# Weights, states and tables stored in device memory in the order in which the partitions read them

## Chip, cores and metric

One core of one Trainium2 chip. The metric is device time in microseconds (us) of one execution, lower is better. It covers the program on the device; what `kernel()` does with arrays on the host before and after is no part of it.

## The reference, cut to what matters

One step of a one-layer hybrid decoder for a prompt of 512 tokens and 8 sample sequences of 8 tokens each, all in fp32, width 1024:

```python
h = RMSNorm(x)
z, xbc, dt, q, kv_c, kv_s, kv_w, nsa_g, br_g = split(h @ w_in)       # 1024 x 9040
y_ssm, conv_new, ssm_new = mamba(z, causal_conv(xbc, state_conv), dt, state_ssm)   # 32 heads, state 128
o_attn, win_new = nsa(q, kv_c, kv_s, kv_w, caches, page_table)       # 16 heads, 2 KV groups
merged = sigmoid(g_ssm) * (y_ssm @ w_ssm_branch) + sigmoid(g_attn) * (o_attn @ w_attn_branch)
x = x + merged @ w_out
x = x + PEER(RMSNorm(x))     # q = h @ peer_wq, scores against peer_sub_keys, 128 experts per token:
                             # out = sum_k gelu(h . peer_u[e_k]) g_k peer_v[e_k],  e_k among 16384
y = RMSNorm(x)
```

Outputs are y, the new key and value rows, the new convolution tails (3 rows of 3072 columns for the prompt and for each sequence) and the new recurrent states (32 heads x 64 x 128 for the prompt and for each sequence).

## The kernel before, in words

Tokens stand in 5 tiles: 0 to 3 hold the prompt, 128 tokens each, and tile 4 the 64 sample tokens. `build` (L3647) runs the chain of stages norm, conv, ssd, zgate, branch, kv, qk, cmp, attn, branch, out, query twice: for group "a" (tiles 0 and 1) and for group "b" (tiles 2, 3 and, for the projections, 4). In names of tiles and tensors the last letter is the group. Then come stages for the sample alone (state, mix, branch, pages, cmp, attn, branch, out, query), and at the end `rest`. Each stage is a Block: all engines meet at its end.

**Weights.** `Weights` cuts the matrices into pieces of [128 partitions x 2048 floats], 1 MB each, and SP loads them in the order of use (`feed`, L3623) into slots: 16 for group a (2 of `wb`, 14 in the ring of the experts, which is idle then), the 2 of `wb` for group b. A slot's next load is issued when the PE has used the piece in it. In DRAM the matrices lie row after row, so that one partition's part of a piece is made of short runs: 1 KB for 256 columns of `w_in`, `w_attn_branch` and `peer_wq`, 512 B for the 128 columns of `w_ssm_branch` (L3588), 256 B for the 64 columns of a query head, where a piece takes 4 DMAs (L3600), 4 KB for `w_out`. The sample's own stages load 2 MB at a time into `wb` and `room` (L2208, L2904, L3007), in runs of 4 or 2 KB.

**Experts.** `Experts` (L3112) interleaves, from group b on, the expert rows of earlier tiles with the stages: 576 gathers of `peer_u` and 576 of `peer_v`, an indirect DMA from GpSimd each (L3314), 128 rows of 4 KB = 0.5 MB, into a ring of 14 slots `e_ring`. The VectorE takes a `u` slot with one dot product (L3463), the PE four `v` slots with 16 matmuls (L3381). How many of them each stage carries is fixed by `k.share`; the stages' hooks (`ex.pe(i)`, `ex.dve(i)`, ...) place them between the stage's own instructions. A gather is issued when the slot 14 places before it has been read. Weights go through DMA queue 1 (issued by SP), gathers through queue 0 (issued by GpSimd).

**Norm** (a): norm weights and convolution weights are loaded as rows, `vec_a` and `vec_b`, and turned by the PE into the columns `vcol` (L277, L255).

**Conv** (b): for each of 24 channel tiles f, the PE projects (L379, 8 matmuls of 320 columns) and turns the old tail from `zs`/`sigs` rows into PSUM (L384); ACT copies to SBUF (L503 to L508); the VectorE convolves and copies the new tail (L561, L562); ACT applies Silu; the PE turns the output (L400) and the new tail (L403); ACT copies both out (L454 to L458). The tails leave as rows from SBUF (L359).

**Ssd** (b): 8 units; the VectorE adds each unit's state into `h` (L824). At the end the PE turns all of `h` in 16 transposes (L750), ACT copies them (L790), and SP stores them in one DMA and waits for it (L844).

**Query** (a): sub keys are loaded as rows (L1719), turned by 16 transposes (L1750) between the second and third projection, copied by ACT (L1808), and stored as `keys_scratch`, from which group b and the sample load them. Scores (L1769) feed the ranking on the VectorE.

**State** (sample): 16 head pairs, in each 0.5 MB of `state_ssm` in and 0.5 MB out, both in runs of 512 B (L1895, L1901), through 8 slots.

Of the kernel before, what the change touches and what calls it, by code (L numbers as in the profile page):

```python
# [116 lines left out]
def stage_norm(nc, k, g):  # L117

    with ExitStack() as ctx:
# [9 lines left out]
        if g.first:  # L129
            vec_a, vec_b = sb("vec_a", [32, P]), sb("vec_b", [120, P])  # L130
            table, part = sb("table", [P, NB], I32), sb("part", [P, 1], I32)
            tablef, partf = sb("tablef", [P, NB]), sb("partf", [P, 1])
            vec_in, table_in, const_set, consts_done, vec_turned, a_done = (
                sem(n) for n in ("vec_in", "table_in", "const_set", "consts_done", "vec_turned", "a_done"))
# [6 lines left out]
        def _(sp):  # L141
# [5 lines left out]
            for dst, src in (  # L147
                (vec_a[0:8, :], k.norm_mix_w[0].rearrange("(a p) -> a p", p=P)),
                (vec_a[8:16, :], k.norm_ffn_w[0].rearrange("(a p) -> a p", p=P)),
                (vec_a[16:32, :], k.ssm_norm_w[0].rearrange("(a p) -> a p", p=P)),  # L150
                (vec_b[0:24, :], k.conv_b[0].rearrange("(a p) -> a p", p=P)),
                (vec_b[24:120, :], k.conv_w[0].rearrange("w (a p) -> (w a) p", p=P)),
# [59 lines left out]
        def _(act):  # L212
# [10 lines left out]
            if g.first:  # L223
                act.wait_ge(vec_in, 16 * 8)
# [3 lines left out]
        def _(dve):  # L228
# [64 lines left out]
def stage_conv(nc, k, g):  # L293


    with ExitStack() as ctx:  # L296
# [13 lines left out]
        TURNS = F if g.sample else B_TILES  # L310
        per = WB // P
        NTP = len(g.prompt)
        if g.sample:
            cin_s = sb("in_s", [P, 2, NB, CONV_W - 1 + DS])
            tail = sb("tail", [P, 2, 27])
            ends_bc = k.sigs[:].rearrange("p a f n -> p (a f n)")[0:27]
            state_in, written = sem("state_in"), sem("written")

        def ends(f, r):

            if f < X_TILES:
                return k.zs[0:r, f * P:f * P + P]
            return ends_bc[0:r, (f - X_TILES) * P:(f - X_TILES) * P + P]
# [25 lines left out]
        def _(sp):  # L349
            if g.sample:  # L350
                state = k.state_conv[0].rearrange("b w c -> (b w) c")
                sp.dma_start(k.zs[0:24, :], state[:, 0:D_INNER]).then_inc(state_in, 16)
                sp.dma_start(ends_bc[0:24, :], state[:, D_INNER:]).then_inc(state_in, 16)
            k.w.feed(sp)
            if g.sample:
                sp.wait_ge(gathered, F)
                after = k.new_conv_sample[0].rearrange("b w c -> (b w) c")
                for src, cols in ((k.zs, slice(0, D_INNER)), (ends_bc, slice(D_INNER, CONV_DIM))):
                    sp.dma_start(k.new_conv_prompt[0, 0][:, cols], src[0:3, :]).then_inc(written, 16)  # L359
                    sp.dma_start(after[:, cols], src[3:27, :]).then_inc(written, 16)  # L360
                sp.wait_ge(written, 64)
# [9 lines left out]
        def _(pe):  # L371
            def project(f):
# [8 lines left out]
                if g.sample:  # L381
                    if f == 0:
                        pe.wait_ge(state_in, 32)
                    last = nc.tensor.transpose(k.ps[:, f % 2, N:N + 24], ends(f, 24), k.ident[0:24, 0:24])  # L384
                last.then_inc(projected, 1)

            def turn(f):
# [3 lines left out]
                if f < B_TILES:  # L391
                    pe.wait_ge(activated, f + 1)
                    for i, t in enumerate(g.tiles):
# [3463 lines left out]
```

## Time and profile before

| what | value |
|---|---|
| median of 3 runs | 3231.45 us (3214.28 to 3235.7) |
| profiled execution, own time | 3234.93 us |
| its span in the trace | 3233.2 us |
| PE busy / VectorE / ScalarE / GpSimd | 2217.7 / 1543.3 / 616.9 / 1492.6 us |
| DMA packets, bytes | 401016, 843.89 MB, mean 261 GB/s |
| queue 0 (gathers), share of 16 DMA engines | 644.95 MB, 54.6% |
| queue 1 (SP), share of 16 DMA engines | 229944 packets, 196.89 MB, 20.4% |

By the first matmul of each stage, group a ends at 708.4 us, group b at 1960.8 us, and the sample's stages and `rest` take what is left. A packet in the profile is one contiguous piece of a DMA. "Share" is the mean busy share of the core's 16 DMA engines, so 0.91 of a stage of 143.8 us is 130.9 us of work for all 16. A row "A <- B: t, n, m" of the waits says that A sat idle t us in n times, the longest m, until B was done.

### The profile page before, as it was taken

Reading aid. Unit: us, or ns where it says so; the run is one execution under the profiler, and the core shown is the slowest. Engines: PE = TensorE matmul, PEld = TensorE weight load, DVE = VectorE, ACT = ScalarE, POOL = GpSimd, SP = SyncE. Lnnn points to the kernel's source line nnn. Section 1 sums busy time; section 2 is a strip of 40 time slices with the busy share of each in tenths; the row PEclk is TensorE's granted clock in tenths of the full one; section 3 lists DMA queues with packets and bytes.
Section 4 is the critical chain, followed back from the end, with each engine's and each line's share of the span. In section 5 each row is a group of like instructions: output and inputs, shape, how many; then the busy total and the mean of one; then the engine's idle time right before and its main releaser. Section 6 shows DMA issues by size and latency. Waiting matters only on the chain. (4 is left out here: it accounts for less than half of the span.)

```text
span 3233.2 us, 32111 instructions
## 1 busy us (share of the span) xinstructions
PE 2217.7 (69%) x11116; PEld 1403.4 (43%) x11116; DVE 1543.3 (48%) x3888; ACT 616.9 (19%) x1746; POOL 1492.6 (46%) x1509
## 2 busy tenths in 40 slices
PE   8999979869777678756688894653446777564044
PEld 7788846556555466422235362332114443111000
DVE  4410042276888751256520065998535665108720
ACT  3330053113331100013340012321001111000000
POOL 0200000053254664457754357657555665443775
PEclk9999969879978888877899996655668898777567
DMA  6234602437637997889989978968988998997998
GB/s 218 79 92 121 140 26 78 130 111 236 204 102 257 332 325 263 266 325 350 350 308 290 349 250 287 352 221 284 412 344 325 352 389 304 314 340 288 339 370 316
DMA packets 401016, 843.89 MB, mean 261 GB/s; under 512 B 71194, under 2 KB 236914, under 8 KB 398181
## 3 DMA queue, kind: packets, MB, share of 16 engines
q0 software_dynamic: 170912, 644.95, 54.6%
q1 hardware_dynamic: 229944, 196.89, 20.4%
q8 instruction: 90, 1.47, 0.2%
q14 instruction: 70, 0.57, 0.1%
HBM read 821.54 MB, written 24.33 MB: 262 GB/s over the span
## 5 line engine op out<-in xcount | busy, mean ns | idle before, releaser
L3314 POOL DMA_INDIRECT e_ring<-in_peer_u,e_idx x576 | 692.2, 1202 | 542.9 <-DVE e_dot L3463 267.4
L3463 DVE CUSTOM_DVE_ANT_0 e_ring<-e_ring,e_h 128x1024 f32<-128x1024 f32 x576 | 703.0, 1254 | 175.4 <-DMA e_ring<-in_peer_u,e_idx 82.4
L3314 POOL DMA_INDIRECT e_ring<-in_peer_v,e_idxT x576 | 583.4, 1013 | 440.3 <-PE ps L3381 178.1
L3381 PE MATMUL ps<-e_ring,e_wz 128*32 128x512 f32 x2304 | 361.5, 742 | 297.1 <-DMA e_ring<-in_peer_v,e_idxT 261.3
L3381 PEld LDWEIGHTS ps<-e_ring,e_wz 128*32 128x32 f32 x2304 | 76.8, 125 | 507.2 <-issue 502.4
L1672 POOL CAST ra_atf<-ra_at 128x32 f32<-128x32 uint32 x8 | 1.7, 211 | 259.7 <-DVE ra_hit L1665 259.7
L379 PE MATMUL ps<-hTb,wb 128*128 128x320 f32 x384 | 112.1, 447 | 1.9 <-DMA wb<-in_w_in 1.9
L1957 PE MATMUL ps<-ss_bsel,ss_xde 64*128 64x512 f32 x64 | 54.6, 947 | 63.1 <-DVE room L2007 27.5
L1004 PE MATMUL ps<-hTb,wb 128*128 128x320 f32 x256 | 77.3, 462 | 16.9 <-DMA wb<-in_w_in 9.6
L379 PEld LDWEIGHTS ps<-hTb,wb 128*128 128x128 f32 x384 | 73.7, 197 | 30.8 <-issue 2.9
L1507 DVE TENSOR_REDUCE apb_nmax<-ps 128x2 f32<-128x768 f32 (+1 forms) x32 | 34.9, 1089 | 105.9 <-PE ps L1431 55.3
L1012 PE MATMUL ps<-xnatb,wb 128*128 128x256 f32 x256 | 66.9, 427 | 24.2 <-DMA wb<-in_w_ssm_branch 24.2
L3506 DVE TENSOR_TENSOR e_x<-e_x,ps 128x512 f32<-128x512 f32 x10 | 6.4, 683 | 155.9 <-PE ps L3381 113.4
L888 PE MATMUL ps<-hTb,wb 128*128 128x320 f32 x256 | 76.8, 456 | 0.0
L1092 POOL MEMSET inda<- 128x256 f32 x1 | 0.3, 312 | 163.6 <-POOLq L3707 163.6
L1012 PEld LDWEIGHTS ps<-xnatb,wb 128*128 128x128 f32 x256 | 55.1, 218 | 36.0 <-DMA wb<-in_w_ssm_branch 25.8
L1004 PEld LDWEIGHTS ps<-hTb,wb 128*128 128x128 f32 x256 | 51.5, 204 | 43.5 <-issue 14.9
L1760 PE MATMUL ps<-hTb,wb 128*128 128x256 f32 x256 | 61.1, 393 | 7.5 <-DMA wb<-in_peer_wq 4.7
L1189 PE MATMUL ps<-hTb,wb 128*128 128x320 f32 x160 | 48.3, 464 | 24.2 <-DMA wb<-in_w_in 17.6
L379 PE MATMUL ps<-hTa,e_ring 128*128 128x256 f32 x288 | 64.9, 379 | 0.0
L656 POOL TENSOR_TENSOR sa_xdt<-xnata,dt 128x512 f32<-128x512 f32 x8 | 8.4, 1044 | 121.3 <-POOLq L296 104.0
L888 PEld LDWEIGHTS ps<-hTb,wb 128*128 128x128 f32 x256 | 50.5, 203 | 20.0 <-issue 3.7
(720 smaller groups left out, 4329.9 us busy)
## 6 DMA issues: line engine op xcount, KB each, us to landing
wb<-in_w_in SPq DMA_DIRECT2D x38, 1024.0 KB, 5.3
e_ring<-in_w_in SPq DMA_DIRECT2D x24, 1024.0 KB, 5.3
wb<-in_peer_wq SPq DMA_DIRECT2D x10, 1024.0 KB, 5.4
wb<-in_w_ssm_branch SPq DMA_DIRECT2D x9, 1024.0 KB, 6.1
e_ring<-in_peer_u,e_idx POOLq DMA_INDIRECT x576
e_ring<-in_peer_v,e_idxT POOLq DMA_INDIRECT x576
e_ring<-in_w_ssm_branch SPq DMA_DIRECT2D x7, 1024.0 KB, 5.8
wb<-in_w_in SPq DMA_DIRECT2D x24, 256.0 KB, 4.3
```

Of the source, the lines that this page charges most:

```text
L379: last = nc.tensor.matmul(k.ps[:, f % 2, 0:N], w[:, kk, c:c + P], k.hT[:, kk, 0:N], start=(kk == 0), stop=(kk == KD - 1))
L656: gp.tensor_tensor(v3(xdt), x3, by_head(k.dt[:, t0 + c, hs], P), ALU.mult).then_inc(xdt_done, 1)
L888: last = mm(k.ps[:, f % 2, 0:N], w[:, kk, :], k.hT[:, kk, 0:N], start=(kk == 0), stop=(kk == KD - 1))
L1004: last = mm(k.ps[:, b, 0:N], w[:, f, :], k.hT[:, f, 0:N], start=(f == 0), stop=(f == KD - 1))
L1012: last = mm(k.ps[:, b + 1, 0:NP], w[:, f, :], src_p(f), start=(f == 0), stop=(f == depth - 1))
L1189: last = nc.tensor.matmul(k.ps[:, i % 4, 0:N], w[:, f, :], k.hT[:, f, 0:N], start=(f == 0), stop=(f == KD - 1))
L1507: v.tensor_reduce(nmax[:, 2 * d:2 * d + 2], k.ps[:, 0:2, 0:width(d)], AX.X, ALU.max, negate=True).then_inc(maxed, 1)
L1760: last = mm(k.ps[:, i % 2, 0:NP], w[:, f, :], k.hT[:, f, 0:NP], start=(f == 0), stop=(f == KD - 1))
L1957: mm(k.ps[:, 2 + q % 2, :], xde[:, f * P:f * P + P], bsel[:, j % 2, seqs(i), :].rearrange("p b n -> p (b n)"), start=True, stop=True).then ...
L3314: nc.gpsimd.indirect_dma_start(out=self.ring[:, place % self.NR, :], out_offset=None, in_=k.peer_u if kind == "u" else k.peer_v, in_offset ...
L3381: last = nc.tensor.matmul(k.ps[32 * b:32 * b + 32, self.SUMS + i, :], self.wz[:, at:at + 32], self.ring[:, self.v_at[n] % self.NR, 512 * i ...
L3463: v.tensor_tensor_reduce(uu, uu, self.h[:, tile % 2, :], 1.0, 0.0, ALU.mult, ALU.add, self.dot[:, tile % 2, t:t + 1]).then_inc(self.dotted, 1)
```

## The change

`kernel()` now hands over, beside the other inputs, arrays in the order in which the program reads them: all pieces of the weights as `weights[n]`, [128, 2048], so that a partition's part of a piece is one run of 8 KB; the sample's copies as `late_weights[n]`, [128, 4096], runs of 16 KB; the five vectors as `columns` [128, 152]; the sub keys turned; `state_ssm` as [16, 128, 1024] with runs of 4 KB, and the same for the new states; the window cache with runs of 4 KB; the convolution states by channel. New states and tails of prompt and sample are stored as they lie in SBUF and put into the reference's order on the host. The on-chip turns of vectors, sub keys, tails and prompt state go.

```diff
@@ Weights
-        for n, loads in enumerate(self.pieces):
-            self.total[n % self.slots] += 16 * len(loads)
+        for n in range(len(self.pieces)):
+            self.total[n % self.slots] += 16
...
-        for i in range(HPK // 2):
-            add([(lambda t, side=side, j=j: pair(t, side, j),
-                  w_view(k.w_in, COL_Q + (side * HPK + 2 * i + j) * HD, HD)) for j in range(2) for side in range(KVH)])
...
-            for part, src in self.pieces[n]:
-                sp.dma_start(part(self.places[n % self.slots]), src).then_inc(self.sem[n % self.slots], 16)
+            width = self.pieces[n]
+            sp.dma_start(self.places[n % self.slots][:, 0:width],
+                         self.k.weights[n][:, 0:width]).then_inc(self.sem[n % self.slots], 16)
@@ stage_norm
-                (vec_a[0:8, :], k.norm_mix_w[0].rearrange("(a p) -> a p", p=P)),
...
+                (k.vcol[:], k.columns),
...
-                    dve.wait_ge(vec_turned, 1)
-                    own(v.tensor_copy(k.vcol[:, 0:32], k.ps[:, 6, 0:32]))
-                    own(v.tensor_copy(k.vcol[:, 32:152], k.ps[:, 7, 0:120]))
+                    dve.wait_ge(vec_in, 16 * 4)
@@ stage_conv
-                sp.wait_ge(gathered, F)
...
+                sp.wait_ge(tailed, F)
+                sp.dma_start(k.new_conv_prompt, k.ctail[:].rearrange("p f t -> p (f t)")).then_inc(written, 16)
+                sp.dma_start(k.new_conv_sample, after.rearrange("p f b t -> p (f b t)")).then_inc(written, 16)
...
-                if g.sample:
-                    if f == 0:
-                        pe.wait_ge(state_in, 32)
-                    last = nc.tensor.transpose(k.ps[:, f % 2, N:N + 24], ends(f, 24), k.ident[0:24, 0:24])
...
-                if g.sample:
-                    pe.wait_ge(tailed, f + 1)
-                    last = nc.tensor.transpose(k.ps[0:27, b, 3 * P:4 * P], tail[:, f % 2, :], k.ident[:])
...
-                    last = a.copy(ends(f, 27), k.ps[0:27, b, 3 * P:4 * P])
...
-                    last = a.copy(cin_s[:, f % 2, :, 0:3], src[:, N:N + 24].rearrange("p (b t) -> p b t", b=NB))
+                    if f == 0:
+                        act.wait_ge(state_in, 16)
+                    last = a.copy(cin_s[:, f % 2, :, 0:3], before[:, f])
@@ stage_ssd
-                        last = nc.tensor.transpose(k.ps[:, q, i * P:i * P + P], h[:, f * P:f * P + P], k.ident[:])
...
-                sp.wait_ge(h_copied, 4)
-                sp.dma_start(k.new_ssm_prompt[0, 0].rearrange("h p n -> (h p) n").rearrange("(f q) n -> q f n", q=P),
-                             hout).then_inc(h_stored, 16)
-                sp.wait_ge(h_stored, 16)
+                for gr in range(GROUPS):
+                    sp.wait_ge(updated, U - GROUPS + gr + 1)
+                    sp.dma_start(k.new_ssm_prompt[:, channels(gr)], h[:, channels(gr)]).then_inc(h_stored, 16)
+                sp.wait_ge(h_stored, 16 * GROUPS)
@@ stage_sample_state
-                sp.dma_start(h0[f % NH0], view(k.state_ssm, f)).then_inc(h0_in[f % NH0], 16)
+                sp.dma_start(h0[f % NH0], k.state_before[f].rearrange("p (b n) -> p b n", b=NB)).then_inc(h0_in[f % NH0], 16)
@@ stage_sample_branch
-                for dst, part in load_w(wp[i % 2], w, i):
-                    sp.dma_start(dst, part).then_inc(wp_in[i % 2], 16)
+                sp.dma_start(k.room[i % 2], k.late_weights[first + i]).then_inc(wp_in[i % 2], 16)
```

The PE's instructions in conv of group b, before (L379 projects, L384 turns the old tail, L400 the output, L403 the new tail):

```order
L379 MATMUL ps<-hTb,wb 128x320 x8
L384 MATMUL ps<-ident,zs 128x24
L379 MATMUL ps<-hTb,wb 128x320 x8
L384 MATMUL ps<-ident,zs 128x24
L400 MATMUL ps<-ident,cb_out 128x128 x2
L400 MATMUL ps<-ident,cb_out 64x128
L403 MATMUL ps<-ident,cb_tail 27x128
L379 MATMUL ps<-hTb,wb 128x320 x8
```

and the same place of the changed kernel:

```order
L383 MATMUL ps<-wb,hTb 64x32 x8
L358 MATMUL ps<-hTb,wb 128x320 x16
L374 MATMUL ps<-ident,cb_out 128x128 x2
L374 MATMUL ps<-ident,cb_out 64x128
L358 MATMUL ps<-hTb,wb 128x320 x8
```

The two small turns of each channel tile are gone; the order of the rest is the same.

The PE's instructions at the end of ssd in group b, before (L720 and L727 belong to the last units, L895 and L888 to zgate):

```order
L708 MATMUL ps<-sb_xdt,zs 128x64 x8
L720 MATMUL ps<-h,mTb 128x512
L727 MATMUL ps<-sigs,Bnatb 128x512
L750 MATMUL ps<-ident,h 128x128 x16
L615 UNCONDITIONAL_BRANCH
L878 UNCONDITIONAL_BRANCH
L895 MATMUL ps<-ident,xnatb 128x128 x2
```

In the changed kernel the row L750 is missing, and nothing else moves there. SP's loads in kv and qk of group b, before (64 columns: one of the 4 DMAs of a query piece):

```order
L3634 DMA wb<-in_w_in 128x8x256
L3634 DMA wb<-in_w_in 128x8x48
L3634 DMA wb<-in_w_in 128x8x64 x8
L1068 UNCONDITIONAL_BRANCH
L1166 UNCONDITIONAL_BRANCH
L3634 DMA wb<-in_w_in 128x8x64 x12
```

and of the changed kernel:

```order
L3558 DMA wb<-in_weights 128x2048
L3558 DMA wb<-in_weights 128x384
L3558 DMA wb<-in_weights 128x2048 x2
L1017 UNCONDITIONAL_BRANCH
L1115 UNCONDITIONAL_BRANCH
L3558 DMA wb<-in_weights 128x2048 x5
```

The loads stand in the same order, one DMA to a piece. GpSimd's instructions are the same in both kernels.

## Rows read from the trace of the kernel before

**Rows 1.** Windows view by stage: length, busy time of each engine, granted clock, DMA share, GB/s.
```profile
0.00:708.40 708.40, 609.54 (x2905) 488.89 (x2905) 216.13 (x683) 196.03 (x566) 71.06 (x143) 0.90 0.37 104
723.80:883.00 159.20, 138.12 (x616) 97.08 (x617) 121.09 (x385) 51.91 (x210) 45.47 (x44) 0.92 0.70 226
1099.60:1243.40 143.80, 109.83 (x404) 83.63 (x405) 68.40 (x125) 8.56 (x23) 79.66 (x60) 0.84 0.91 312
1243.40:1376.90 133.50, 103.34 (x464) 67.03 (x464) 31.02 (x52) 9.16 (x35) 61.00 (x61) 0.87 0.84 265
1691.10:1801.40 110.30, 92.01 (x437) 57.05 (x433) 6.77 (x16) 4.53 (x20) 43.65 (x49) 0.92 0.91 288
1960.80:2164.50 203.70, 133.24 (x448) 75.59 (x449) 174.13 (x429) 58.20 (x165) 135.24 (x121) 0.64 0.96 324
2250.40:2304.30 53.90, 23.72 (x75) 7.02 (x77) 32.85 (x60) 1.45 (x5) 35.33 (x31) 0.69 1.03 410
2778.20:3233.20 455.00, 186.50 (x968) 48.05 (x968) 162.53 (x442) 22.01 (x54) 258.28 (x268) 0.70 0.90 335
```

**Rows 2.** DMA view of 1126 to 1130 us: packets, MB, share of the 16 engines.
```profile
q0 software_dynamic: 341, 1.23, 78.9%
q1 hardware_dynamic: 341, 0.35, 24.9%
```

**Rows 3.** DMA view of 1102 to 1104 us, where queue 1 stores an 8 KB row per partition.
```profile
q1 hardware_dynamic: 92, 0.49, 62.3%
```

**Rows 4.** DMA view of 17 to 120 us: loads with 1 KB runs, no gathers.
```profile
q1 hardware_dynamic: 19007, 19.17, 59.5%
```

**Rows 5.** DMA view of 335 to 345 us: loads with 256 B runs, no gathers.
```profile
q1 hardware_dynamic: 4160, 1.05, 59.3%
```

**Rows 6.** DMA views of 1100 to 1243, 1243 to 1376 and 1692 to 1801 us, queue 1.
```profile
q1 hardware_dynamic: 18847, 12.16, 28.6%
q1 hardware_dynamic: 24916, 8.54, 27.8%
q1 hardware_dynamic: 6712, 7.96, 26.9%
```

**Rows 7.** Waits of the engines from 1100 to 1243 us: total, times, longest.
```profile
PE ps L1012 <- DMA wb<-in_w_ssm_branch: 24.2, 4, 8.8
PE ps L1004 <- DMA wb<-in_w_in: 7.9, 2, 5.4
```

**Rows 8.** Waits from 1244 to 1376 us.
```profile
PE ps L1189 <- DMA wb<-in_w_in: 17.6, 1, 17.6
```

**Rows 9.** Waits from 1692 to 1801 us.
```profile
PE ps L1012 <- DMA wb<-in_w_attn_branch: 14.8, 3, 5.2
```

**Rows 10.** Waits from 2251 to 2304 us and from 2779 to 3010 us.
```profile
PE ps L2223 <- DMA wb<-in_w_ssm_branch: 24.8, 2, 20.0
PE ps L2223 <- DMA wb<-in_w_attn_branch: 13.9, 1, 13.9
```

**Rows 11.** Windows view of 1126.5 to 1131.5 us, just behind a wait for weights.
```profile
1126.50:1131.50 5.00, 5.00 (x12) 4.01 (x13) 0.00 (x0) 0.00 (x0) 1.88 (x2) 0.50 1.04 394
```

**Rows 12.** Groups of instructions from 723.8 to 883 us, shapes apart.
```profile
L384 PE MATMUL ps<-ident,zs 24*128 24x24 f32 x16 | 3.8, 239 | 0.0
L403 PE MATMUL ps<-ident,cb_tail 128*27 128x128 f32 x24 | 6.8, 283 | 8.2 <-DVE cb_tail L562 8.2
```

**Rows 13.** Timeline of TensorE around 628 us: start, length, instruction.
```profile
628.28 1.04 PE L1750 MATMUL ps<-ident,ra_sk 128*128 128x128 f32 x8
631.37 0.71 PE L1769 MATMUL ps<-ra_skT,ra_qT 128*128 128x128 f32 x4 [0.68 <-ACT ra_skT L1808]
```

**Rows 14.** Timeline of VectorE around 973 us.
```profile
972.89 0.68 DVE L824 TENSOR_TENSOR h<-h,ps 128x512 f32<-128x512 f32 x1
983.57 1.23 DVE L3463 CUSTOM_DVE_ANT_0 e_ring<-e_ring,e_h 128x1024 f32<-128x1024 f32 x1 [10.00 <-PEq L615]
```

**Rows 15.** Waits of GpSimd in the whole span.
```profile
POOL e_ring L3314 <- DVE e_dot L3463: 312.7, 112, 11.5
```

More of the change, by code:

```diff
@@ L314, in stage_conv @@
             cin_s = sb("in_s", [P, 2, NB, CONV_W - 1 + DS])
-            tail = sb("tail", [P, 2, 27])
-            ends_bc = k.sigs[:].rearrange("p a f n -> p (a f n)")[0:27]
             state_in, written = sem("state_in"), sem("written")
[L319 to L323, printed above, removed]
+            before, after = (k.zs[:, D * i:D * i + F * NB * (CONV_W - 1)].rearrange("p (f b t) -> p f b t", f=F, b=NB)
+                             for i in range(2))
         NT, t0 = len(g.tiles), g.tiles[0]
@@ L537, in convolve @@
                     dve.wait_ge(activated, f - 1)
-                    if g.sample:
-                        dve.wait_ge(turned, f - 1)
                 ap = acc[:, f % 2, 0:NP]
@@ L743, in _ @@
                     ex.pe(2 * u + 1)
-            if g.sample:
-                pe.wait_ge(updated, U)
-                pe.wait_ge(y_half, U)
-                for q in range(4):
-                    for i in range(4):
-                        f = 4 * q + i
-                        last = nc.tensor.transpose(k.ps[:, q, i * P:i * P + P], h[:, f * P:f * P + P], k.ident[:])
-                    last.then_inc(h_turned, 1)
         @block.scalar
@@ L785, in _ @@
                     ex.act(2 * u + 1)
-            if g.sample:
-                act.wait_ge(diag, U)
-                for q in range(4):
-                    act.wait_ge(h_turned, q + 1)
-                    a.copy(hout[:, 4 * q:4 * q + 4, :],
-                           k.ps[:, q, :].rearrange("p (i n) -> p i n", i=4)).then_inc(h_copied, 1)
         @block.vector
@@ L1717, in store @@
                 sp.dma_start(k.scores_dram[t0][:, i, :], s[:, i % NS_BUF, 1, :]).then_inc(s_out[i % NS_BUF], 16)
-            sp.dma_start(*((sk[:], keys) if g.first else (skT[:], k.skT_dram))).then_inc(sk_in, 16)
+            sp.dma_start(skT[:], k.keys_turned).then_inc(sk_in, 16)
             for i in range(HC):
@@ L1804, in _ @@
                     a.copy(qT[:, i % 2, :], k.ps[:, i % 2, 0:NP]).then_inc(q_copied, 1)
-                if i == 1 and g.first:
-                    for q in range(HC // 4):
-                        act.wait_ge(sk_turned, q + 1)
-                        a.copy(skT[:, 4 * q:4 * q + 4, :],
-                               k.ps[:, 2 + q % 2, :].rearrange("p (i n) -> p i n", i=4)).then_inc(sk_copied, 1)
                 if i:
@@ L2167, in stage_sample_mix, with stage_sample_branch @@
         ex.close()
-def row_chunk(dst, w, i):
-    return [(dst, w[512 * i:512 * i + 512, :].rearrange("(f p) n -> p f n", p=P))]
-def head_chunk(dst, w, i):
-    return [(dst[HD * g:HD * g + HD], w.rearrange("(g j d) n -> g d j n", g=KVH, d=HD)[g][:, 4 * i:4 * i + 4])
-            for g in range(KVH)]
-def stage_sample_branch(nc, k, name, w, depth, load_w, src, which):
+def stage_sample_branch(nc, k, name, first, depth, src, which):
     with ExitStack() as ctx:
```

245 lines of the change are left out of this document (119 added, 126 removed).

## The prediction

> **What bounds the kernel now.** I read the windows view stage by stage first. In group a, the first 708.4 us, TensorE works 609.5 us, the DMA share is 0.37 and no gathers run [rows 1]: here the PE sets the time, and faster loads buy nothing. From group b on the gathers run, and most stages show a DMA share of 0.84 to 1.03 [rows 1]. In the branch stage, 143.8 us, the PE works 109.8 and the DMA engines 0.91 x 143.8 = 130.9 us; both attention projections and the late stages look alike. State is different: VectorE works 174.1 of 203.7 us.
>
> The waits come second. In branch the PE waits 24.2 + 7.9 = 32.1 us for pieces of weights [rows 7], in kv and qk once for 17.6 us, for a query piece [rows 8], in the attention's branch 14.8 us [rows 9], in the sample's branch stages 24.8 and 13.9 us [rows 10].
>
> The DMA view tells why. At 1126 to 1130 us both queues moved 341 packets: they take turns, one packet for one packet, whatever a packet holds [rows 2]. So gathers with 4 KB packets got 1.23 MB through and weights, in runs of 1 KB, 0.35 MB: 88 GB/s, which makes a piece of 1 MB last 12 us, and one in runs of 512 B twice that, while the PE needs about 7 us for 16 matmuls of 427 ns. Where nothing contends, runs of 1 KB move 19.17 MB in 0.595 x 103 us of all engines, 19.5 GB/s an engine [rows 4]; runs of 256 B move 1.05 MB in 5.9 us, 11 GB/s an engine [rows 5]; the one place with 8 KB rows, a store beside gathers, shows 62.3% of the engines for queue 1 and 0.49 / (0.623 x 2 x 16) = 24.6 GB/s an engine [rows 3], 394 GB/s for 16. That is the nearest row for the new layout.
>
> So long runs do two things: a piece costs the engines less (1 MB: 2.7 us of all 16 instead of 3.4 with 1 KB and 5.9 with 256 B), and, which matters more, it arrives sooner beside gathers (1 MB at 0.49 MB in 2 us: 4.3 us, instead of 12 or more). With 8 KB packets a piece is never late for a PE that needs 7 us for one, unless its slot comes free late: each slot waits for the PE's use of the piece before, and two slots are enough for 4.3 us.
>
> A rule speaks against half of this. The Trainium skill, "DMA: Bandwidth & Descriptors", section Specifications, gives 512 B as the smallest transfer for full rate; by it only the 256 B pieces and the states' smallest rows would gain throughput. Rows 4 disagree, 19.5 against 24.6 GB/s at 1 KB, though not by much. What it would make of the time is rival 3.
>
> **The change part by part.** The sum is made against the profiled execution's own time, 3234.93 us (span 3233.2), which is 3.5 us over the median of the runs shown.
>
> Start-up (vectors as one load, no turns): two turns of the nearest row's size, 0.28 us each [rows 12], and two copies go, and the one load in place of several must still land first. 0 taken; -2 to +2.
>
> Key turns in group a's query: the PE goes from L1750 at 628.28 to the first scores at 631.37 us [rows 13]: the two quarters of turns seen there and the copy behind them go, and 631.37 - 628.28 = 3.1 us with them. **3**; 2 to 4. The keys of group b already come turned; their runs change little, 0.
>
> Conv of group b: out go 24 turns of the old tail at 239 ns and 24 of the new at 283 ns, 5.7 + 6.8 us, and of the 8.2 us that the PE waits for the VectorE's copy of the tail [rows 12]. At most 20.7. ACT gives up two copies a tile, which were beside. The PE works 138.1 of 159.2 us and VectorE 121.1 [rows 1], so a stage without the turns may run at 138.1 - 12.5 = 125.6, but hooks and the VectorE's chain (conv, Silu, turn) remain, and part of the turns lies in waits that stay. I take half, **10**; 3 to 20.
>
> End of ssd of group b: VectorE finishes its last sum at 973.57 and has nothing till 983.57 us, the next stage [rows 14]. In these 10 us the PE turns the whole state, ACT copies it and one DMA of 1 MB stores it. Now each of 4 quarters is stored behind its last update; only the last, 0.25 MB, is exposed. It takes at least 0.25 / 0.394 = 0.7 us and surely less than the whole gap, in which turns, copies and four times the bytes fit; I take 4. 10 - 4 = **6**; 3 to 9. Group a's state isn't stored.
>
> Branch of group b: PE waits are 32.1 us. The floor by the engines: queue 1 took 0.286 x 143 = 40.9 us for 12.16 MB [rows 6]; at 394 GB/s they take 30.9, 10.0 less, so the stage needs 120.9 us of all engines. 143.8 - 120.9 = 22.9 against 32.1 of waits: the engines bind. A little of the stage's end has no transfers at all. **21**; 8 to 30.
>
> kv and qk: wait 17.6; queue 1 took 0.278 x 133 = 37.0 us for 8.54 MB, the query pieces among them in 256 B runs; at 394 GB/s 21.7, so the engines need 0.84 x 133.5 - 15.3 = 96.8 and the PE 103.3 us of 133.5. Neither binds before the wait is used up. **18**; 10 to 22.
>
> The attention's branch: wait 14.8; queue 1 from 29.3 to 20.2 us; the engines need 0.91 x 110.3 - 9.1 = 91.3, the PE 92.0 us. **14**; 6 to 18.
>
> The PE's clock adds to these terms: behind a wait of 8.8 us it was granted 0.50, 1.2 GHz, for 5 us [rows 11]; each long wait that goes gives back up to 2.5 us. I count this into the upper ends.
>
> State: 16 MB in and out had runs of 512 B and get 4 KB. The share of 0.96 falls, but VectorE's 174.1 us stay, with 203.7 - 174.1 = 29.6 us beside them, in which the gathers and slots are waited for. **5**; 0 to 20.
>
> The sample's weights, 2 MB a load, had runs of 4 or 2 KB and get 16 KB. They wait 38.7 us in all in two of the stages [rows 10], but these run at shares of 1.03 and 0.90: a load that gains its turns takes them from gathers that the same stages must carry. A third of 38.7, **12**; 0 to 30.
>
> Remaining loads in query of b, window cache, output weights and zgate: **4**; 0 to 10.
>
> Sum: 3 + 10 + 6 + 21 + 18 + 14 + 5 + 12 + 4 = 93; 3234.9 - 93 = **3142 us**. All lower ends together give 3235 - 30 = 3205; all upper ends 3235 - 165 = 3070, which would need every guess to err the same way.
>
> **The rivals.**
>
> Rival 1: engines, not arrival. Gathers that lose their turns to long weight packets come later, and the PE or VectorE waits for them in place of weights. Then a stage gains only what the packing saves: 10.0 + 15.3 + 9.1 = 34 us in the three stages, of which some is not bound, about 28; with 19 from the turns and ssd, and 8 from state and sample, 55: **3180 us**. For it speak shares of 0.91 to 1.03; against it a share of 0.84 in kv and qk, where the engines have room, and that in branch both counts end near each other.
>
> Rival 2, the slower side: starved gathers. While an 8 KB load is under way, queue 1 takes 62.3% of the engines [rows 3] and gathers keep 38%, in place of 79% [rows 2]; a load lasts 4.3 us, so 0.623 x 4.3 = 2.7 us of gathering is lost to each of the 59 loads of group b. If the ring ran dry each time this would be waited for in full: 59 x 2.7 = 159 us, less the 93 gained, 66 slower: **3301 us**. It decides when the ring of 14 slots holds less than 2.7 us of work as a load starts. Against it: GpSimd waits 312.7 us in 112 waits for VectorE to free a slot [rows 15], so the ring is full at most times, and the same bytes are moved in all, so what gathers lose now they get back when no weights are loading.
>
> Rival 3: long runs give no rate and no earlier arrival, since 512 B is enough. Then only the 256 B pieces gain (14 us, most of the one wait of 17.6), and the removed turns and the ssd end, 19 to 20: **3201 us**. Against it stand rows 2, where packets and not bytes are shared out, and rows 4.
>
> Rival 4: everything hidden behind the waits comes out. All 32.1 + 17.6 + 14.8 + 38.7 = 103 us of waits go, 19 of turns and ssd and some 8 of clock: **3105 us**. Against it: the engines' floor in branch and the shares near 1 in the sample's stages.
>
> **How the numbers follow.** My forecast 0.5, rival 1 0.2, rival 4 0.15, rival 3 0.11, rival 2 0.04. A measurement of this kernel tells a change of about 1%, 32 us, from none. The forecast, rival 1 and rival 4 are all faster than 3199; rival 3 lies at the bound and counts as the same, less a small part of it: faster 0.86, same 0.10, slower 0.04. The range runs from 3072, a little short of all upper ends, to all lower ends, 3205 us; it takes in rivals 1, 3 and 4 and leaves out rival 2.
>
> **What would show it.** In the changed profile, queue 1 should read 8 KB packets, fewer than a third of the 229944 packets, and a share well below 20.4% for the same bytes; in branch, kv and the attention's branch the PE's waits for weights should be gone or under 5 us each, and a granted clock of 0.84 in branch should rise above 0.90; branch should last about 123 us, kv and qk 115, the attention's branch 96. Conv should last 149, VectorE's gap at the end of ssd 4 us, state 199. If rival 1 holds, the waits of PE and VectorE for `e_ring` grow by what the weights' waits lose. If rival 2 holds, GpSimd no longer waits for slots and VectorE waits for gathers in every stage. If the branch stages keep their waits though packets are 8 KB, my reading of turns packet by packet is wrong. Group a should stay within 5 us of 708.4; a larger gain there would mean that loads bound it after all, where I see a busy PE.

## The result, and the profile after

The changed kernel took 3102.4 us (median of 4), the kernel before 3227.6 us in the same comparison: a ratio of 0.9616, 95% interval 0.956 to 0.967. In a later session, in which both were faster (3021.3 and 3146.1 us), the ratio was 0.9591 (0.9564 to 0.9617). The forecast was 3142 us with a range of 3072 to 3205; the gain was 125 us where I had summed 93. The change did what it says: of the 401016 packets 209128 are left, and queue 1 carries nearly the same bytes with a share of 17.0% in place of 20.4%.

The page's line on packets and its queues (packets, MB, share):

```profile
DMA packets 209128, 842.83 MB, mean 271 GB/s; under 512 B 25609, under 2 KB 32073, under 8 KB 189449
q0 software_dynamic: 170912, 644.95, 55.9%
q1 hardware_dynamic: 38056, 195.83, 17.0%
```

The windows of after, stage by stage (columns as in [rows 1]): group a, conv of group b, branch, kv with qk, the attention's branch, state, and the last stages.

```profile
0.00:697.40 697.40, 601.28 (x2886) 481.91 (x2886) 215.36 (x681) 193.85 (x562) 71.53 (x143) 0.92 0.30 105
711.80:867.70 155.90, 131.21 (x569) 93.29 (x570) 121.11 (x385) 48.97 (x186) 45.50 (x44) 0.91 0.66 231
1077.80:1194.00 116.20, 98.80 (x405) 75.29 (x405) 69.05 (x125) 8.66 (x23) 76.54 (x60) 0.93 0.98 384
1194.00:1292.50 98.50, 94.73 (x464) 61.74 (x464) 30.92 (x52) 9.15 (x35) 61.13 (x61) 1.00 0.94 357
1605.50:1692.00 86.50, 84.67 (x436) 52.39 (x432) 6.77 (x16) 4.52 (x20) 42.50 (x48) 1.00 0.98 364
1851.30:2057.60 206.30, 134.19 (x448) 76.43 (x449) 173.30 (x429) 58.21 (x165) 138.39 (x122) 0.63 0.88 319
2661.00:3111.60 450.60, 186.17 (x968) 47.39 (x968) 162.49 (x442) 22.01 (x54) 265.44 (x272) 0.68 0.90 341
```

Stage by stage, in the two profiled executions (3234.93 and 3113.39 us, 121.5 us apart):

| part | before, us | after, us | saved | forecast |
|---|---|---|---|---|
| group a, the key turns among it | 708.4 | 697.4 | 11.0 | 3 |
| norm and conv of b | 174.6 | 170.3 | 4.3 | 10 |
| ssd of b | 100.5 | 93.9 | 6.6 | 6 |
| branch of b | 143.9 | 116.2 | 27.7 | 21 |
| kv and qk of b | 133.5 | 98.5 | 35.0 | 18 |
| attention's branch of b | 110.2 | 86.6 | 23.6 | 14 |
| state | 203.8 | 206.3 | -2.5 | 5 |
| the sample's other stages and the rest | 1068.7 | 1054.1 | 14.6 | 12 |
| all others (zgate, cmp, attention, out, query of b) | | | 1.2 | 4 |

Three stages hold 86 of the 121.5 us. The waits for weights there are all but gone. From 1077.8 to 1194 us, where [rows 7] had 24.2 and 7.9 us, TensorE waited so (A <- B: us, times, longest):

```profile
PE ps L3283 <- DMA e_ring<-in_peer_v,e_idxT: 10.2, 1, 10.2
PE ps L961 <- DMA wb<-in_weights: 2.8, 2, 1.7
```

and in qk, against [rows 8]:

```profile
PE ps L1138 <- DMA wb<-in_weights: 1.4, 1, 1.4
```

The first row of branch is new: one wait of 10.2 us for a gather. Some of what the weights gained there was handed to the experts, which is the mechanism of rival 1 at about a third of the 32.1 us. Over the whole kernel its sign shows too: TensorE's waits for gathered `peer_v` rows went from 261.3 to 290.3 us (272.8 in w_only below, where only the prompt's weights changed), VectorE's for `peer_u` rows from 82.4 to 122.6 us (some 20 us of this rise may be one wait of 19.3 us in state; before had one of 21.6 us there, which the view puts down to "issue"). GpSimd still waits for slots, 285.2 us on VectorE and 141.8 on TensorE in place of 312.7 and 211.3, so the ring doesn't run dry as rival 2 had it. How pieces arrive, shown by the queues from 1100 to 1104 us (packets, MB, share), with [rows 2] beside it:

```profile
q1 hardware_dynamic: 136, 0.99, 59.8%
q0 software_dynamic: 179, 0.66, 40.5%
```

1 MB in 4 us for queue 1, which I had bounded with a store's row at 4.3 [rows 3]. The turns are only about packet for packet: 34 of these 315 packets, and 41 of the 682 in [rows 2], are small ones under 512 B. By the bytes, 121 packets of 8 KB passed here beside 161 of 4 KB, and 341 of 1 KB beside 300 of 4 KB in [rows 2].

### The profile page after: what moved, and what is told of

Same layout as the page of the kernel before. It is cut to its first block and busy times, and to the rows that moved or that the text cites. A ratio compares the mean times of both kernels' runs of the same rounds, so it can differ in the third digit from the quotient of the medians.

```text
span 3111.7 us, 31861 instructions
## 1 busy us (share of the span) xinstructions
PE 2169.4 (70%) x11034; PEld 1374.2 (44%) x11034; DVE 1540.9 (50%) x3886; ACT 609.7 (20%) x1714; POOL 1495.0 (48%) x1509
## 2 busy tenths in 40 slices
DMA packets 209128, 842.83 MB, mean 271 GB/s; under 512 B 25609, under 2 KB 32073, under 8 KB 189449
## 5 line engine op out<-in xcount | busy, mean ns | idle before, releaser
L3365 DVE CUSTOM_DVE_ANT_0 e_ring<-e_ring,e_h 128x1024 f32<-128x1024 f32 x576 | 701.3, 1249 | 165.6 <-DMA e_ring<-in_peer_u,e_idx 122.6
L3283 PE MATMUL ps<-e_ring,e_wz 128*32 128x512 f32 x2304 | 363.7, 747 | 316.7 <-DMA e_ring<-in_peer_v,e_idxT 290.3
L358 PE MATMUL ps<-hTb,wb 128*128 128x320 f32 x384 | 114.0, 454 | 0.0
L358 PEld LDWEIGHTS ps<-hTb,wb 128*128 128x128 f32 x384 | 75.3, 201 | 30.1 <-issue 4.9
L953 PE MATMUL ps<-hTb,wb 128*128 128x320 f32 x256 | 73.8, 447 | 8.3 <-PEq L804 7.3
L837 PE MATMUL ps<-hTb,wb 128*128 128x320 f32 x256 | 77.2, 458 | 0.0
L1690 PE MATMUL ps<-hTb,wb 128*128 128x256 f32 x256 | 62.8, 401 | 7.2 <-DMA wb<-in_weights 4.4
L953 PEld LDWEIGHTS ps<-hTb,wb 128*128 128x128 f32 x256 | 49.4, 196 | 33.9 <-issue 15.5
L961 PE MATMUL ps<-xnatb,wb 128*128 128x256 f32 x256 | 57.3, 383 | 4.2 <-DMA wb<-in_weights 2.8
L1883 PEld LDWEIGHTS ps<-ss_h0t,ss_cmask 128*64 128x64 f32 x256 | 42.8, 195 | 39.6 <-issue 34.8
L837 PEld LDWEIGHTS ps<-hTb,wb 128*128 128x128 f32 x256 | 50.7, 203 | 20.3 <-issue 4.3
L1690 PEld LDWEIGHTS ps<-hTb,wb 128*128 128x128 f32 x256 | 49.7, 199 | 22.0 <-issue 9.3
```

Source lines behind the costliest of these rows:

```text
L358: last = nc.tensor.matmul(k.ps[:, f % 2, 0:N], w[:, kk, c:c + P], k.hT[:, kk, 0:N], start=(kk == 0), stop=(kk == KD - 1))
L837: last = mm(k.ps[:, f % 2, 0:N], w[:, kk, :], k.hT[:, kk, 0:N], start=(kk == 0), stop=(kk == KD - 1))
L953: last = mm(k.ps[:, b, 0:N], w[:, f, :], k.hT[:, f, 0:N], start=(f == 0), stop=(f == KD - 1))
L961: last = mm(k.ps[:, b + 1, 0:NP], w[:, f, :], src_p(f), start=(f == 0), stop=(f == depth - 1))
L1690: last = mm(k.ps[:, i % 2, 0:NP], w[:, f, :], k.hT[:, f, 0:NP], start=(f == 0), stop=(f == KD - 1))
L1883: last = mm(k.ps[0:NS, 5, fj * P:fj * P + P], cmask[:, j, HB * i + b, :], h0t[:, q % 2, b, :], start=(i == 0 and b == 0), stop=(i == 1 and ...
```

## The experiments

Each is compared with the kernel before in its own session; where two kernels are compared, it is by these ratios or by stages of their profiles. Stages whose code is the same differ a little from one profile to the next: branch took 112.5 to 116.2 us in the five profiles with the changed kernel's weights and shares (after, after_again, w_only, late_old2, state_512b), and the sample's out stage 41.2 to 49.3 us in the ten with the change's own form of it.

**old_runs** and **small_runs2**: the changed kernel, pieces in the old run lengths. Shortened, from old_runs; small_runs2 takes its 512 B and 256 B pieces from arrays in which all pieces' runs of the same number lie together.

```diff
-            sp.dma_start(self.places[n % self.slots][:, 0:width], self.k.weights[n][:, 0:width])
+            dst = dst.rearrange("p (c w) -> p c w", c=c)
+            src = self.k.weights[n].rearrange("a b -> (a b)").rearrange("(c p w) -> p c w", c=c, p=P)
+            sp.dma_start(dst, src)      # c = 8, 16, 32 or 2 runs a partition
```

> The changed kernel, but each piece of the prompt's weights lies in DRAM in the run lengths of before (1 KB, 512 B for the SSM branch, 256 B for the queries, 4 KB for w_out), still dense and still one DMA a piece. Theory, run length sets both the engines' cost and the pieces' arrival beside gathers: branch, kv with qk and the attention's branch go back to about 144, 133 and 110 us, 86 us in all, and the kernel takes about 3190 us (3175 to 3205). Rival, not the runs but what came with them helped (one DMA in place of four, dense blocks in place of rows 36 KB apart): it stays under 3130 us.

Measured: 3170.0 us, ratio 0.9792 (0.9755 to 0.9829), so 57 us of the 124 were lost, between theory and rival. Branch took 137.7 us, kv 46.1, qk 73.5, the attention's branch 103.7. But the trace shows that the kernel is not what I meant it to be. Its line on packets:

```profile
DMA packets 302310, 842.81 MB, mean 265 GB/s; under 512 B 25608, under 2 KB 130376, under 8 KB 297992
```

No 256 B packets of weights are in it, and 512 B runs came as 2 KB, 256 B runs as 1 KB: a run of partition p is followed in DRAM by the run of partition p + 1, and one packet took four of them. Moving the runs of one partition farther apart, with the same neighbours, changed nothing:

> As old_runs, but there the trace shows packets of 2 KB for the 512 B runs and of 1 KB for the 256 B runs, four neighbouring runs in one packet; here the runs of a piece lie 288 or 512 KB apart, so that each should be a packet of its own. Still one DMA a piece. Theory, the number of packets sets the arrival: branch 143, kv with qk 121 to 130 (the 192 B piece stays whole, which was worth 12 us), attention's branch 104 to 110, in all 3190 us (3175 to 3205), above old_runs. Rival, the layout's other sides (four DMAs, rows 36 KB apart) made the rest of the loss: as old_runs, 3170 us or less.

Measured: 3167.2 us, ratio 0.9779 (0.9726 to 0.9832), the same packets (302311), branch 137.8 us. Here the rival's number came out, but for a reason that neither side had: the packets had never been restored. The sentence ahead of the prediction, that a packet is one contiguous piece of a DMA, is too simple; it can hold several partitions' runs where these touch.

**runs_1k** and **runs_4k**: c = 8 or 2 for all full pieces.

> All full pieces in runs of 1 KB. Theory: 256 B and 512 B pieces are mended, 1 KB pieces still get a fifth of the bandwidth beside gathers, so about half of the 86 us is lost: 3145 us (3125 to 3165), with waits for weights of 5 to 20 us left in branch and some in kv and qk. Rival, 512 B or more is enough for full rate: within 1% of the changed kernel, under 3133 us, and branch at 116 us.

> All full pieces in runs of 4 KB, as long as the gathers' packets, so each queue gets half while both are busy: a piece in 5.2 us, still faster than the PE uses one (7 to 8 us). Theory, a piece only has to arrive before the PE needs it: within 8 us of the changed kernel, 3095 to 3115. Rival, the weights have to win over the gathers as they do with 8 KB: 15 us or more slower, 3120 us or more, with waits for weights back in branch.

Measured: 1 KB 3151.0 us, ratio 0.9731 (0.9687 to 0.9775); 4 KB 3105.6 us, ratio 0.9616 (0.9564 to 0.9668), equal to the changed kernel. Branch with 1 KB and with 4 KB:

```profile
1082.90:1214.60 131.70, 106.61 (x405) 81.09 (x405) 68.31 (x125) 8.59 (x23) 80.15 (x60) 0.90 0.95 339
```
```profile
1073.40:1185.90 112.50, 99.91 (x405) 76.74 (x405) 68.72 (x126) 8.60 (x23) 82.86 (x60) 0.95 1.01 390
```

The rival for 1 KB falls: 131.7 us, not 116, with 23.0 us of waits for weights. The rival for 4 KB has its waits, but not its price. In branch TensorE waited so for weights, and not at all for a gather:

```profile
PE ps L953 <- DMA wb<-in_weights: 6.3, 2, 3.2
PE ps L961 <- DMA wb<-in_weights: 3.8, 2, 3.2
```

So a piece did not always come before it was needed, as the theory had it: 10.1 us of waits for weights with 4 KB stand against 2.8 for weights and 10.2 for a gather with 8 KB. With the engines at shares of 1.01 and 0.98, the run length only settles who waits. From 4 KB up nothing is left to win here. The Trainium skill, "DMA: Bandwidth & Descriptors", Specifications, gives 512 B as the smallest transfer for full rate. The measurement says otherwise for this load: 1 KB against 8 KB is 15.5 us in this one stage. Most of that is the engines' own work: queue 1 took 27.8% of 131.7 against 26.3% of 116.2 us, 6.0 less, and the gathers 66.9 against 71.1%, 5.5 less. The other 4 us are idle time of the engines.

**runs_apart**: the old packets at last. Every run is followed by 256 unused bytes.

```diff
+            out[c, width] = np.zeros((c, len(pieces_like(n)), P, width // c + 64), np.float32)
...
+            src = self.k.spread[runs_key(n)][:, pieces_like(n).index(n)].rearrange("c p w -> p c w")[:, :, 0:w]
```

> The changed kernel with the weights' packets as before, the 192 B and 128 B pieces among them, made so that they stay single: each run is followed by 256 unused bytes, so that runs of neighbouring partitions don't touch. One DMA a piece, no rows 36 KB apart. Theory, the number and size of packets is the whole of it: 229944 packets less the states' and late ones, branch 140 to 146 us, kv 55 to 59, qk 72 to 77, attention's branch 107 to 112, and the kernel 85 to 100 us above the changed one, all that w_only gained. Rival, merged DMAs or the dense layout hold the part that old_runs and small_runs2 left open: 65 us above it or less.

> The changed kernel once more, so that the three beside it are compared with it on one chip. Nothing is tested; 3095 to 3120 us.

Measured, in one session: the changed kernel 3021.3 us, ratio 0.9591 (0.9564 to 0.9617); runs_apart 3109.0 us, ratio 0.9879 (0.9848 to 0.991). The 3095 to 3120 us expected of the changed kernel were missed because that session was faster for every kernel. 87.6 us lie between the medians (91 by the ratios), in the theory's 85 to 100; the two profiled executions, the fastest of runs_apart and the slowest of the changed kernel, are 69.6 us apart. The packets, and branch, kv with qk, and the attention's branch:

```profile
DMA packets 385767, 842.83 MB, mean 272 GB/s; under 512 B 103432, under 2 KB 222024, under 8 KB 381448
q1 hardware_dynamic: 214696, 195.83, 20.7%
```
```profile
1075.20:1212.40 137.20, 106.34 (x405) 80.97 (x405) 68.53 (x125) 8.57 (x23) 79.30 (x60) 0.88 0.93 327
1212.40:1331.80 119.40, 106.81 (x464) 69.29 (x464) 31.06 (x52) 9.26 (x35) 62.12 (x61) 0.89 0.96 296
1622.10:1731.00 108.90, 89.88 (x435) 55.34 (x432) 6.76 (x16) 4.52 (x20) 43.48 (x49) 0.91 0.88 296
```

Branch falls just short of the theory (137.2 where 140 was the lower end), kv (53.2) and qk (66.2) by 2 and 6 us. There a query piece was four DMAs before and is one here. The gap at the end of kv, 6.6 us before, is 0.9 us here with the old packets, so it belongs to the four DMAs and not to the packets; for qk no run tells the two apart. The three stages took 365.6 us here, 298.2 in the changed kernel of the same session and 387.6 in the kernel before (of the other session): the packets hold 67 of these 89 us. That is most of the gain, and up to 22 us may lie in the rest of the layout or in the session.

**w_only**: the kernel before with the changed `Weights`, nothing else.

> The kernel before with the prompt's weights alone laid out in runs of 8 KB; turns, stores, states, the sample's weights as before. Theory: the three stages give their 86 us and group a some 5, so 3227 - 91 = 3136 us (3125 to 3150), and the remaining 30 us or so of the change lie in the other parts. Rival, the turns and the stores were worth more than their stages show (what they free is used elsewhere): slower than 3155 us.

Measured: 3142.0 us, ratio 0.9706 (0.9664 to 0.9748), by the ratio 95 us below the kernel before. Its branch is that of the changed kernel:

```profile
1091.80:1208.00 116.20, 98.93 (x405) 75.09 (x405) 69.02 (x125) 8.63 (x23) 75.53 (x60) 0.93 0.97 385
```

The parts add up: 95 us from the prompt's weights, and some 30 us (0.9706 against 0.9616, with intervals that leave it open by some 20) from all the rest. Conv of b took 159.6, ssd 100.5 and query of a 88.7 us here, as before, so what these three gave, 13 to 14 us, is the turns' and the stores'. runs_apart, which has all the rest and the old packets, is 38 us faster than the kernel before; of these, 22 lie in the three stages of the weights, as said above, and 16 elsewhere.

**warm2**: the kernel before, with matmuls that nobody reads ahead of the waits in both branch stages.

```diff
+            def idle_work(bank, width, n):
+                for _ in range(n if g.sample else 0):
+                    mm(k.ps[:, bank, 0:width], k.ident[:], k.hT[:, 0, 0:width], start=True, stop=True)
...
-                pe.wait_ge(*k.w.here(i))                          # in gate: behind the other wait and the filling
+                idle_work(b, N, ({2: 8, 6: 16} if per == 3 else {2: 6}).get(m, 0))
+                pe.wait_ge(*k.w.here(i))
...
+                idle_work(b + 1, NP, ({1: 36, 3: 28, 5: 8, 7: 20} if per == 3 else {2: 20, 4: 20, 6: 20}).get(m, 0))
```

> The kernel before, with extra matmuls (into the bank that the next piece's result takes) where the PE waits for weights in branch and in the attention's branch, nearly as long as each wait, 36 to 6 of them a place. Theory, arrival paces these stages and the low clock behind a wait only fills what would be waiting: granted clock near 1.00, branch still 140 to 146 us, attention's branch 108 to 112, total within 5 us of before. Rival, the low clock is a cost of its own: branch 11 us and attention's branch 7 us shorter, total 3212 us or less.

Measured: 3248.5 us, ratio 1.0049 (1.0019 to 1.0078), branch 149.4 and the attention's branch 115.7 us. Windows, and the groups of branch (count | busy us, mean ns; L999 is the filling, L1018 projects):

```profile
1095.30:1244.70 149.40, 147.47 (x637) 119.19 (x637) 68.56 (x125) 8.60 (x23) 78.34 (x60) 0.98 0.87 302
1687.30:1803.00 115.70, 113.86 (x568) 77.49 (x564) 6.77 (x16) 4.53 (x20) 42.11 (x48) 1.00 0.87 272
```
```profile
L1018 PE MATMUL ps<-xnatb,wb 128*128 128x256 f32 x256 | 56.7, 379 | 0.0
L999 PE MATMUL ps<-hTb,ident 128*128 128x256 f32 x184 | 40.4, 379 | 0.0
L999 PE MATMUL ps<-hTb,ident 128*128 128x320 f32 x48 | 13.2, 432 | 0.0
```

The clock came to 0.98 and 1.00, and the projections' 256 matmuls took 56.7 us where they had taken 66.9. But the filling is twice as long as I meant: each matmul stands in the trace as two, so it took 40.4 + 13.2 = 53.6 us against 32.1 us of waits, and TensorE itself paced the stage. Neither side is shown for the two stages. What it does show is that without waits the clock stays up here. The stage behind it, kv, has the code and the packets of before and shows something of the clock's price. It began at full clock and without its wait of 3.8 us, and took 49.2 us where it had taken 58.3:

```profile
1244.70:1293.90 49.20, 42.85 (x241) 30.21 (x241) 12.31 (x20) 4.17 (x13) 29.56 (x33) 0.97 0.99 316
```

The same 241 matmuls took 42.9 in place of 47.8 us, 5.0 of the 9.1 us. The gap at the stage's end was still there, 6.3 us.

**late_old2** and **state_512b**: the changed kernel with the sample's weights, or its states, in the old runs.

```diff
-                sp.dma_start(k.room[i % 2], k.late_weights[first + i])
+                sp.dma_start(k.room[i].rearrange("p (c w) -> p c w", c=c), src)      # c = 4, w_out 8
...
-                sp.dma_start(h0[f % NH0], k.state_before[f].rearrange("p (b n) -> p b n", b=NB))
+                sp.dma_start(h0[f % NH0], k.state_before[:, f].rearrange("b p n -> p b n"))
```

> The changed kernel with the sample's weights back in runs of 4 KB (2 KB for w_out), nothing else. Theory, those loads gained what I summed for them: 12 us slower, 3110 to 3120 us, most of it in sample out (43 back to 56 us). Rival, these stages are bound by the sum of all transfers, and who goes first doesn't matter: within 4 us of the changed kernel.

> The changed kernel with the sample's states in and out in runs of 512 B, the reference's order. Theory, VectorE paces this stage: the DMA share rises from 0.88 to about 0.96, the stage stays 202 to 209 us, the kernel within 5 us of the changed one. Rival, the states' packets also delay gathers that later stages wait for: 10 us or more slower, in state or in mix.

Measured: 3114.1 us, ratio 0.9615 (0.9563 to 0.9667), and 3112.8 us, ratio 0.9635 (0.9586 to 0.9685). Neither is apart from the changed kernel's 0.9616. The states' stage, and the sample's out stage in late_old2 and in the changed kernel:

```profile
1843.20:2046.50 203.30, 133.33 (x449) 75.64 (x449) 173.53 (x429) 58.22 (x165) 134.79 (x122) 0.63 0.96 324
```
```profile
2707.30:2763.40 56.10, 33.38 (x138) 9.18 (x138) 2.86 (x5) 2.27 (x6) 26.74 (x30) 0.77 0.92 330
```
```profile
2707.50:2750.40 42.90, 27.50 (x141) 7.93 (x138) 2.85 (x5) 2.27 (x6) 28.91 (x33) 0.90 1.01 401
```

State is as the theory had it: the share is back at 0.96, the stage took 203.3 us. Out lost the 13 us that were expected of it, 56.1 against 42.9 (but up to 49.3 in kernels that left it alone). The last stages took 356.7 against 361.3 us, and the total didn't move beyond its interval. Whether the sample's long runs are worth 0 or 10 us stays open.

**retune1** and **retune2**: the changed kernel with gathers moved to stages with room.

```diff
-    k.share = dict(norm=2, conv=34, ssd=16, zgate=56, bs=58, ... query=38,
+    k.share = dict(norm=2, conv=34, ssd=16, zgate=52, bs=50, ... query=50,     # retune1
+    k.share = dict(norm=2, conv=34, ssd=22, zgate=56, bs=48, ... query=42,     # retune2
```

> The changed kernel with gathers moved out of stages that now run at a DMA share of 0.98 (branch, 58 to 50 expert steps) or at VectorE's limit (zgate 56 to 52) into query, whose share is 0.64 (38 to 50). Theory, branch is now bound by the engines: it gets 8 x 1.43 = 11 us shorter, zgate 2 to 4, query at most 8 longer, the kernel 5 to 14 us faster. Rival, branch is at TensorE's limit (98.8 of 116 us) or query grows as much: within 3 us.

> The changed kernel with branch from 58 to 48 steps, ssd, whose DMA share is 0.35, from 16 to 22, query from 38 to 42. Theory: branch 12 to 14 us shorter, ssd 0 to 6 longer (VectorE works 73 of 94 us), query 0 to 3 longer, the kernel 5 to 12 us faster. Rival, ssd is a chain of short steps, in which each dot product delays the next: ssd 8 us or more longer and nothing gained.

Measured: 3030.7 us, ratio 0.9614 (0.9587 to 0.9641), and 3025.5 us, ratio 0.9594 (0.9565 to 0.9622), against 0.9591: nothing gained, and in retune1 perhaps 7 us lost, within the intervals. Branch and query of the first, ssd and branch of the second:

```profile
1070.70:1178.70 108.00, 98.13 (x388) 76.38 (x388) 63.87 (x117) 9.28 (x25) 68.26 (x50) 0.94 0.93 358
1694.50:1822.30 127.80, 97.55 (x513) 68.52 (x513) 57.64 (x249) 17.29 (x45) 70.17 (x112) 0.85 0.66 242
```
```profile
862.80:969.20 106.40, 72.22 (x320) 56.84 (x321) 86.47 (x180) 33.12 (x130) 58.67 (x57) 0.74 0.38 123
1081.30:1192.00 110.70, 100.11 (x404) 77.45 (x404) 59.05 (x109) 8.68 (x23) 67.19 (x49) 0.94 0.93 357
```

Beside them the changed kernel had branch 113.6, query 110.0 and ssd 93.7 us. So 8 steps less gave branch only 5.6 us and 10 steps less 2.9, where it varies by 3.7 by itself; TensorE's 98 to 100 us now lie close below it, with 7.1 to 8.5 us of waits for weights. Query took 17.8 more for 12 steps; in ssd 6 steps cost 12.7. Both rivals hold, the first with a loss where it had named none. Room at the DMA engines is no room in a stage whose own chain sets its length.

## Why the prediction was right, and where its sum was not

**The mechanism held.** Queues take turns about by packet, so long packets bring weights sooner, and they cost the engines less; the ring of gathers bears it. That arrival counts more than the engines' work, as the prediction says, is not shown: in branch the engines' work fell by 17.3 us and their idle time by 10.4 (from the shares below). The range of 3072 to 3205 us takes in three of the four rivals, so the stages and not the total speak for the mechanism. Rival 3 (512 B suffice) falls with runs_1k, rival 2 with the result. Rival 1 is there in small: the 10.2 us wait for a gather in branch. Rival 4 named 3105 us, and the result came next to it by luck: conv gave less, and the extra came out of terms that it hadn't. One reading was wrong without harm. TensorE's need of 7 us a piece was got from 16 matmuls of 427 ns, but a matmul stands in the trace as two records, and 427 ns is the length of one record, which overlaps the next. The timeline has the 32 records of a piece in 7.07 us at full clock and 9.68 us behind a wait.

**Branch, 27.7 where 21 was summed.** Two parts of the floor were off. Queue 1 went from 28.7% of 143.8 to 26.3% of 116.2 us, 41.3 to 30.6 us, 10.7 where 10.0 was worked out. But the gathers got cheaper too, which I had held constant: 62.0% of 143.8 = 89.2 us became 71.1% of 116.2 = 82.6 us for nearly the same bytes (32.62 and 32.32 MB). The share rose from 0.91 to 0.98 besides.

**kv and qk, 35.0 where 18 was summed.** This is the step that was mis-sized most, and it had two faults. First, TensorE's floor of 103.3 us was read from a stage whose clock the waits themselves had lowered. Before and after:

```profile
1243.40:1301.70 58.30, 47.84 (x241) 33.13 (x241) 11.90 (x20) 4.07 (x13) 29.69 (x33) 0.89 0.84 269
1301.70:1376.90 75.20, 55.49 (x224) 33.90 (x224) 19.12 (x32) 5.10 (x22) 31.31 (x28) 0.86 0.85 263
```
```profile
1194.00:1237.70 43.70, 42.81 (x241) 30.23 (x241) 11.89 (x20) 4.05 (x13) 28.63 (x31) 1.00 0.87 316
1237.70:1292.50 54.80, 51.92 (x224) 31.52 (x224) 19.02 (x32) 5.10 (x22) 32.51 (x31) 1.00 0.99 390
```

With the granted clock at 1.00, the level of 2.4 GHz, the same 464 matmuls took 94.7 us, 8.6 less, and since TensorE now sets these stages' length that counts in full. In the attention's branch it was 7.3 us more (92.0 to 84.7), three quarters of what I missed there. I had named the clock and put it into the upper ends alone; 16 us of it belonged into the sum.

Second, the end of kv. TensorE stood 6.6 us there, and I took the row for the usual gap between stages. It is SyncE, still issuing the four DMAs of a query piece (timeline; 1295.12 is the first of four):

```profile
1295.12 6.02 SPq L3634 DMA_DIRECT2D wb<-in_w_in  x4
1301.66 0.87 PE L1189 MATMUL ps<-hTb,wb 128*128 128x320 f32 x1 [6.58 <-PEq L1068]
```

The view of `wb` by tile gives how long one issue took (ns, least/median/most), before and after:

```profile
L3634 SPq DMA_DIRECT2D wb<-in_w_in x18: 367/983/9057, 1257.9 to 1342.2; - x18
```
```profile
L3558 SPq DMA_DIRECT2D wb<-in_weights x6: 328/328/332, 1206.8 to 1257.2; - x6
```

An issue of 256 B runs took up to 9.06 us. The 18 issues of before took 39 us of SyncE together, the 6 of after 2 us; in runs_apart, with the same short runs in one DMA a piece, none took over 4.35 us. So for kv and qk: waits 17.6 + 3.8 (the second, in kv, isn't in the prediction), clock 8.6, the stage's end 6.6 - 0.9, together 35.7, less 1.4 us of waits that remain.

**Conv, 3.3 of 10.** Turns and the wait for the tail went, 20.7 us by [rows 12], but VectorE's work in the stage, the experts' among it, was untouched: 121.1 us before and after, 5 us for each of the 24 tiles. TensorE now ends its part early and stands 11.50 us at the stage's end, where it had stood 4.4, behind the last tiles and the two stores of the tails:

```profile
864.61 0.34 SPq L338 DMA_DIRECT2D out_new_conv_prompt<-ctail  x1
864.99 0.43 SPq L339 DMA_DIRECT2D out_new_conv_sample<-zs  x1
867.69 0.59 PE L650 MATMUL ps<-later,identb 128*128 128x512 bf16 x1 [11.50 <-PEq L286]
```

I took half as a guess where the same profile had VectorE's work per tile to read. That VectorE paces the rest of the stage is argued from these rows and not tested.

**Ssd, 6.6 of 6.** VectorE's gap at the end is 2.60 us in place of 10.00 [rows 14]:

```profile
958.30 0.68 DVE L773 TENSOR_TENSOR h<-h,ps 128x512 f32<-128x512 f32 x1
961.58 1.23 DVE L3365 CUSTOM_DVE_ANT_0 e_ring<-e_ring,e_h 128x1024 f32<-128x1024 f32 x1 [2.60 <-PEq L579]
```

**Keys, 3.2 of 3.** The scores (L1699) follow the projections (L1690) without a gap, against [rows 13]:

```profile
620.99 3.62 PE L1690 MATMUL ps<-hTa,wb 128*128 128x256 f32 x16
624.45 0.61 PE L1699 MATMUL ps<-ra_skT,ra_qT 128*128 128x128 f32 x4
624.89 3.62 PE L1690 MATMUL ps<-hTa,wb 128*128 128x256 f32 x16
```

**Group a otherwise**: 7.8 us more, where I had said that it would stay within 5 us of 708.4, since loads don't bind there. ssd took 53.5 in place of 57.7 us, branch 86.7 of 88.9, kv with qk 63.6 of 66.9, the attention 2.4 more. It isn't the packets: runs_apart, with the old ones, ends its group a at 694.0 us. Branch, kv and qk of group a do follow the change of `Weights`: 155.8 and 155.5 us in the two kernels without it (before, warm2), 150.1 to 150.2 in w_only, runs_apart and the changed kernel. What in it gives these 5.5 us is open. ssd and the attention of group a took 53.5 to 58.4 and 89.4 to 94.4 us over all the kernels run, with no order in it that I can see.

**State** as forecast in kind, nothing in size: -2.5 us. That VectorE (173 of 206 us) sets it agrees with state_512b, where the share rose and the stage didn't grow.

## What to carry to other kernels

Where a small, urgent stream and a large, patient one share the DMA engines, look at the packets: here each got turns about by packet, so runs as long as the other stream's (4 KB) were what the urgent one needed, and more brought nothing. When a wait goes, work the floor of the stage out with the full clock, not with the busy time that the waits have stretched; and read how long the issuing engine takes for a DMA of short runs, since a long issue can hold up the end of a stage though no engine waits for its data. Free DMA time in a stage is no reason to move work there as long as another engine's chain sets its length.

## What was not expected of the hardware

- An issue of a DMA with 256 B runs on SyncE took 0.37 us at best and up to 9.06 us where several followed one another; with 8 KB runs 0.33 us each. That a full queue holds the issue up is my reading, no run tests it.
- Runs of 256 and 512 B that touch from one partition to the next went four to a packet, also where a partition's own runs lay 288 and 512 KB apart; with 256 B between them they went singly. Runs of 1 KB stayed single though they touch (runs_1k, 11654 packets for 12.19 MB in branch). A 2 KB packet took 112 ns (median) where most are of four such runs, in old_runs, and 84 ns in the changed kernel, where they are single.
- The gathers' own work fell from 89.2 to 82.6 us in branch when the other queue's packets grew.
- In the last session both kernels were 2.5% faster, on a chip of the same number (12) as in the session of old_runs, where the kernel before took 3235.1 us. The changed kernel's attention stages of prompt and sample took 249 and 301 us there and 274 and 349 us in the first profile, most others the same within 3 us. Why is open; only ratios can be compared between sessions.
- The attention's branch took 90.5 us in runs_1k and 103.7 us in old_runs, with runs of 1 KB for its pieces in both. Why is open.
